# Twelve weight slabs of the first projection stored in another column order and read back by other access patterns

## What is computed

```python
SPLIT_SIZES = (ML_QK, ML_QK, ML_WIDTH, ML_WIDTH, ML_WIDTH, ML_HEADS, ML_HEADS,
               HG_FDIM, HG_FDIM, HG_WIDTH, HG_WIDTH)
...
        u = rmsnorm(h, norm_w[l])
        proj = jnp.einsum('bsd,dc->bsc', u, w_in[l].astype(jnp.float32))
        (ml_q, ml_k, ml_v, ml_o, ml_z, ml_i, ml_f,
         hg_q, hg_f, hg_i, hg_g) = jnp.split(proj, split_points, axis=-1)
```

## Time and profile before

| | |
|---|---|
| runs | 1983.43 and 1983.77 us, median 1983.6 |
| span of the profiled execution | 1982.4 us (the runs are 1.0 and 1.4 us above it) |
| PE busy | 1973.1 us, 100% |
| PE weight loads (beside the matmuls) | 1642.8 us, 83% |
| DVE busy | 1476.6 us, 74% |
| ACT busy | 1147.5 us, 58% |
| DMA | 535.95 MB, mean 270 GB/s |
| matmuls | 9126, of them 1536 in the 16 slabs of phase A |

### The profile page before, as it was taken

The page is one execution under the profiler, slowest core; times in us unless marked ns, Lnnn a source line. Parts: engine busy times, 40 slices in busy tenths (PEclk is TensorE's granted clock), DMA queues, the critical chain, the costliest instruction groups (busy, mean ns, idle before and its releaser), DMA issues.

```text
span 1982.4 us, 23547 instructions
## 1 busy us (share of the span) xinstructions
PE 1973.1 (100%) x9126; PEld 1642.8 (83%) x9126; DVE 1476.6 (74%) x1571; ACT 1147.5 (58%) x1417; POOL 114.5 (6%) x140
## 2 busy tenths in 40 slices
PE   9999999999999999999999999999999999999999
PEld 7888888888888888888888888888888888888887
DVE  6877776555666666768888657888988898888764
ACT  7546444554466455556666445666666666666553
POOL 1000010000001110000000000000000000000000
PEclk9999999999999999999999999999999999999999
DMA  9788798999889999858797876788878887877553
GB/s 377 255 250 278 234 322 275 323 327 313 278 287 298 342 341 299 255 195 253 283 299 244 313 242 238 236 299 278 273 229 303 271 264 240 308 251 235 209 178 125
DMA packets 86816, 535.95 MB, mean 270 GB/s; under 512 B 10417, under 2 KB 11185, under 8 KB 40753
## 3 DMA queue, kind: packets, MB, share of 16 engines
q1 hardware_dynamic: 72736, 458.69, 60.9%
q0 software_dynamic: 13824, 75.50, 20.0%
q10 hardware_dynamic: 144, 0.26, 0.0%
HBM read 529.69 MB, written 105.38 MB: 320 GB/s over the span
## 4 chain that ended last, share of the span: by engine, by line
PE 96%; DVE 2%; DMA 1%; ACT 1%; issue 0%; SPq 0%; DVEq 0%; ACTq 0%
PE acc L1342 45%; PE acc L1347 22%; PE aux L1699 15%; PE aux L1703 8%; PE aux L1325 1%; PE aux L1415 1%; DMA raw<-in_w_in 1%; DVE wlo L1851 1%; PE aux L1780 0%; DVE wlo L2507 0%; ACT whi L915 0%; PE aux L1405 0%; PE aux L1430 0%; DVE att_z L2353 0%; PE aux L1316 0%
## 5 line engine op out<-in xcount | busy, mean ns | idle before, releaser
L1851 DVE TENSOR_TENSOR wlo<-raw,whi 128x1024 fp32r<-128x1024 f32 x512 | 624.2, 1225 | 359.7 <-ACT whi L915 350.2
L915 ACT ACTIVATE whi<-raw 128x1024 fp32r<-128x1024 f32 x511 | 537.3, 1058 | 535.0 <-PE acc L1347 490.0
L1342 PE MATMUL acc<-whi,actA_hi 128*128 128x512 f32 x892 | 351.6, 394 | 0.0
L1342 PE MATMUL acc<-whi,actA_lo 128*128 128x512 f32 x892 | 347.4, 390 | 0.0
L1342 PE MATMUL acc<-whi,actB_hi 128*128 128x512 f32 x796 | 312.7, 393 | 0.2 <-DVE actB_lo L2624 0.2
L1342 PE MATMUL acc<-whi,actB_lo 128*128 128x512 f32 x796 | 309.9, 389 | 0.0
L1164 ACT ACTIVATE whi<-ple 128x1024 fp32r<-128x1024 f32 x192 | 202.3, 1060 | 136.0 <-PE acc L1347 87.4
L2507 DVE TENSOR_TENSOR wlo<-ple,whi 128x1024 fp32r<-128x1024 f32 x192 | 231.9, 1223 | 37.6 <-ACT whi L1164 30.6
L1347 PE MATMUL acc<-wlo,actA_hi 128*128 128x512 f32 x892 | 238.7, 389 | 0.0
L1347 PE MATMUL acc<-wlo,actB_hi 128*128 128x512 f32 x796 | 213.2, 390 | 1.2 <-DVE wlo L1851 1.2
L2507 DVE TENSOR_TENSOR wlo<-raw,whi 128x1024 fp32r<-128x1024 f32 x144 | 175.4, 1223 | 36.1 <-ACT whi L1164 30.9
(11 more groups left out here) (360 smaller groups left out, 2391.9 us busy)
## 6 DMA issues: line engine op xcount, KB each, us to landing
raw<-in_w_in SPq DMA_DIRECT2D x108, 1024.0 KB, 7.6
raw<-in_w_ffn_out SPq DMA_DIRECT2D x44, 1024.0 KB, 7.0
summed<-in_w_ffn_in POOLq DMA_DIRECT2D x36, 1024.0 KB, 11.9
raw<-in_w_ffn_in SPq DMA_DIRECT2D x72, 512.0 KB, 7.5
ple<-summed SPq DMA_DIRECT2D x24, 1024.0 KB, 4.8
raw<-summed SPq DMA_DIRECT2D x48, 512.0 KB, 4.8
ple<-in_w_ffn_in SPq DMA_DIRECT2D x18, 1024.0 KB, 7.6
ple<-in_w_ffn_in POOLq DMA_DIRECT2D x36, 512.0 KB, 9.8
```

The source lines that it names most:

```text
L915: act.activation(whi[:, g % RING], raw_piece(g), ACT.Copy).then_inc(hi_ready, 1)
L1342: pe.matmul(acc2(n)[:, t, :], act[x][:, k + c, t * P:(t + 1) * P], whi[:, g % RING, c, :], start=(p == 0 and c == 0 and x == 0), stop=False)
L1851: dve.tensor_tensor(wlo[:, g % RING], raw_piece(g), whi[:, g % RING].bitcast(F32), ALU.subtract)\
```

## The change

The host now stores the columns of slabs 1 to 7 and 9 to 13 in another order within the slab, the same in every row. The table `READ_ORDER` gives three numbers h, g, e for a slab: the 512 columns are seen as g groups of h runs of e columns, and stored with the h index outermost. The matmul's moving operand is the same 512 words of `whi` or `wlo`, now walked in the order g, h, e, which is the reference's order again. So for slab 9, (2, 256, 1), word 0 is followed by word 256, then 1, then 257; for slab 10, (256, 2, 1), by words 2, 4, up to 510, and then the odd ones; for slab 1, (2, 64, 4), four words are read at 0, four at 256, four at 4, and so on. Slabs 0, 8, 14 and 15 and all other weights are read as before. On each engine the instructions, their order and their waits stay as they are, 96 matmuls of each of the twelve slabs have the new pattern.

```diff
--- before.py
+++ after.py
@@ -79,6 +79,19 @@
 
 HG_START = (23, 49)
 X_SQUARES = 11
+
+READ_ORDER = {1: (2, 64, 4), 2: (2, 32, 8), 3: (2, 16, 16), 4: (2, 8, 32), 5: (4, 32, 4), 6: (2, 128, 2), 7: (8, 16, 4),
+              9: (2, 256, 1), 10: (256, 2, 1), 11: (4, 8, 16), 12: (16, 8, 4), 13: (2, 4, 64)}
+
+
+def in_read_order(x, order):
+
+    h, g, e = order
+    if order == (256, 2, 1):
+        return x.rearrange("p (g h) -> p h g", h=2)
+    if e == 1:
+        return x.rearrange("p (h g) -> p g h", h=h)
+    return x.rearrange("p (h g e) -> p g h e", h=h, g=g)
 ATT_START = (35, 55)
 
 
@@ -1330,6 +1343,11 @@
                 if u >= 4:
                     aux_taken(pe, u - 4)
 
+            def moving(ring, n, g, c):
+
+                x = ring[:, g % RING, c, :]
+                return in_read_order(x, READ_ORDER[n]) if n in READ_ORDER else x
+
             def piece(n, p, act, k, last, i=0, slabs=0):
 
                 g = SLABS[n][p]
@@ -1339,12 +1357,12 @@
                 for c in range(PK):
                     for t in range(T):
                         for x in range(2):
-                            pe.matmul(acc2(n)[:, t, :], act[x][:, k + c, t * P:(t + 1) * P], whi[:, g % RING, c, :],
+                            pe.matmul(acc2(n)[:, t, :], act[x][:, k + c, t * P:(t + 1) * P], moving(whi, n, g, c),
                                       start=(p == 0 and c == 0 and x == 0), stop=False)
                 pe.wait_ge(lo_ready, g + 1 + i * ROUND)
                 for c in range(PK):
                     for t in range(T):
-                        ins = pe.matmul(acc2(n)[:, t, :], act[0][:, k + c, t * P:(t + 1) * P], wlo[:, g % RING, c, :],
+                        ins = pe.matmul(acc2(n)[:, t, :], act[0][:, k + c, t * P:(t + 1) * P], moving(wlo, n, g, c),
                                         start=False, stop=(last and c == PK - 1))
                 ins.then_inc(piece_used, 1)
 
@@ -2770,7 +2788,15 @@
     for name in _WEIGHTS:
         laid[name] = blocks(inputs[name][0])
     w = inputs["w_in"][0]
-    laid["w_in"] = blocks(np.concatenate([w[:, :MI], w[:, HQ:]], axis=1))
+    laid["w_in"] = blocks(np.concatenate([w[:, :MI], w[:, HQ:]], axis=1)).copy()
+    for s, (h, g, e) in READ_ORDER.items():
+        slab = A_COLS[s] // COLS if A_COLS[s] < MI else (A_COLS[s] - HQ) // COLS + MI // COLS
+        x = laid["w_in"][slab]
+        if (h, g, e) == (256, 2, 1):
+            x = x.reshape(*x.shape[:-1], 2, 256).swapaxes(-1, -2)
+        else:
+            x = x.reshape(*x.shape[:-1], g, h, e).swapaxes(-2, -3)
+        laid["w_in"][slab] = x.reshape(laid["w_in"][slab].shape)
     laid["w_in_gates"] = w[:, MI:HQ].reshape(KD, P, HQ - MI).transpose(1, 0, 2)
     for name in ("w_pe", "w_ple_2"):
         laid[name] = short(inputs[name][0])
```

## The result

The changed kernel takes 2033.5 us in the median of 2 runs (2032.37 and 2034.70), 1.0244 of the time before, with a 95% interval of 1.0227 to 1.026. That is 49.9 us more, where 20.5 were forecast. The time lies inside the range (1982.5 to 2046), but it is slower by more than the 2% that the forecast kept within, between rivals B2 (2024.6) and B (2045.0). What the profile shows is none of the cases.

A forecast was written before the change was run, and what follows sets the result against it. PE was taken to bound the kernel, busy 1973.1 of 1982.4 us. Span 1982.4 plus 20.5 for slab 9, 0 for all else, gave 2002.9; with 1.2 us above the span, 2004.1 us; range 1982.5 to 2046.

The forecast's parts named there:

- B2: Moving reads of slabs 9 and 10 double, slab 6 is free: +41.0 us, 2024.6 us, 2.07% slower; chance 0.08.
- B: Moving reads with runs under four columns (slabs 6, 9, 10) double, 20.5 us each: 2045.0 us, 3.1% slower; chance 0.17.
- What bounds the kernel: PE busy 1973.1 of 1982.4 us at full clock, so slower matmuls in the first projection lengthen the whole run.
- the zeros for loads, splits, outputs and storage: DMA loads, ACT and DVE splits and PSUM outputs of the rearranged slabs were each priced at cost 0.
- The price of a slab that can't be fed: Streaming part of a slab's 96 matmuls doubles, 213.3 ns more each: 20.5 us a slab.
- Which slabs?: Slab 9 alone, having no column near its predecessor, pays +20.5 us (ends 0 and +31.4); the other eleven pay 0.
- The other floor: Line 1627's matmuls, with one jump in the moving operand, last 377 to 379 ns: one jump costs nothing that shows.
- A gain is excluded: PE already takes a column per cycle in the matmuls, so the lower end of the change's cost is 0.
- A: PE's moving reads run ahead far enough to hide single words, so the change costs nothing: 1983.6 us; chance 0.24.
- C: Each jump between runs in the twelve slabs costs 0.417 ns: 77.8 us more, 2061.4 us, 3.9% slower; chance 0.08.
- D: Every rearranged slab doubles, as PE reads ahead only along the stored row: 245.8 us more, 2229.4 us; chance 0.05.
- The test named in the prediction: If slabs 1, 5, 7 and 12 part from each other, distance counts, not the run, and no case is right.

## Why the prediction was wrong

*What bounds the kernel* held: what the slabs lost went to the end undiminished, 48.0 us in the slabs and 48.2 in the span. So did the zeros for loads, splits, outputs and storage (the ratio of the version that is only stored in the new orders is 1.000), and PE's waits did not grow.

*The price of a slab that can't be fed* was right in size: 20.5 us forecast, 21.5 measured for slab 10. The rows that it was taken from, a write of DVE that doubled with runs under four words, may have nothing to do with it: as far as the runs show, the agreement in size is luck. The factor of two here is that of one word for each line and reader.

**The step that failed is "Which slabs?"** I gave the doubling to slab 9, as the walk farthest from every free row, and zero to the eleven others. The runs showed the opposite: slab 9 gains 1.1 us, slab 10 loses 21.5, slab 6 9.9, and eight others 0.8 to 4.7 each, 17.7 together (slab 11 in part by its low clock). The nearness of two successive columns was the wrong measure. Every second column is what counts: slab 9's are neighbours, slab 10's are four words apart. That rule accounts for these two slabs; the other 27.6 us, of slab 6 and the eight others, are shown to lie in the walk (but for the 1.6 of slab 11's low clock), and why each costs what it does stays open (below). The free reads of DVE by every other word could not carry the argument to PE, as I had said myself of their pace, and then used them all the same to put slab 10 among the free.

The other floor, that a jump costs nothing at line 1627, could not carry it either. I compared durations, which I had just said are not the price, and these matmuls are of another kind: their operands are plain float32 (`sgu_v`, `wsT`), not float32r, and their starts are 0.215 us apart for 256 columns (eight take 1.89 us), 0.84 ns a column, half the pace of the matmuls that were changed. A slower read could hide behind that.

```profile
832.58 1.89 PE L1627 MATMUL aux<-sgu_v,wsT 128*128 128x256 f32 x8
```

*"A gain is excluded"* failed as well, in a small thing. I had 13.4 ns a matmul beyond the 512 columns in hand and took them as fixed. 11 of them hang on the walk, and over the whole program they are 4% of the time.

*The rule of the Trainium skill* (SBUF — State Buffer, section "Door 1: The DMA port swizzle", on lines of 16 bytes and two hits in one) gave slab 9 as the payer, too. The trace disagrees: 216 ns there, and 451 in slab 10, which has two hits in each line, one after the other. The measurement decides. With "two hits" counted for every second column, the rule's number two fits the walks of single words: one gives 451, two 227. The stricter sentence on the same page, a penalty at each crossing, fails in slab 9, which crosses with each column.

*The rivals.* A, no cost, is out. B had slabs 6, 9 and 10 doubled: two of the three lose, 9 does not. B2 had slab 10 right and slabs 6 and 9 wrong; its 2024.6 us was nearest in time, by the wrong sum. C, a price by jump, would give slab 9 its 20.5. D is out with slab 13. The test named in the prediction, that slabs 1, 5, 7 and 12 part from each other, came true (2.3, 3.4, 4.7, 1.9 us), and with it that none of the cases had it. But they do not differ "in their jump alone", as I wrote: they have 2, 4, 8 and 16 rows in turn, so the test does not single out the distance.

**What stays open.** Slabs 1 to 5, 7 and 12 have two words in a line for each reader and should take 227 ns by the rule; they take 236 to 278. In the run with other distances, runs of 4 took 225 ns with 32 rows 16 words apart and 232 with 64 rows 8 apart. Whether the distance between rows or their number makes these differences, which stay within about 50 ns, no run separates.

The six walks with runs of 2 (431 to 487 ns) all have four lines or more for each reader, which puts them in the slow group, but no order within it was found. Nor was the reason why slab 6, where each reader takes turns between two lines and finds two words in each, takes 332 ns, between the two levels, or why four rows in turn take 268 to 283 and not 216.

There is no measurement of a walk of the output in PSUM in place of the order in memory, nor of an odd number of rows in turn. And no walk was shifted by a word or two, so that the groups of four words are aligned ones is assumed.

## What to carry to other kernels

With float32r operands, look at every second column of the moving operand, not at neighbours. In these runs of 512 columns, one of its words in a group of four doubled the matmul, two in succession gave the contiguous pace or, in runs with jumps, up to about 50 ns more, and four in succession saved 11 ns. This kernel, whose PE is never idle, took 80 us less (4%) with its weights stored as two rows and walked in turn; 7 us more of waits were the one cost that showed. And where a trace has a remainder per instruction beyond the array's time, price it as something that could move either way; I took it for a constant.

## What the runs showed of the hardware that was not expected

- A contiguous float32r walk is not the fastest: 227 ns for 512 columns against 216 for two rows in turn, and at 384 columns the difference is nearly the same (173 against 163), so it doesn't go with the columns.
- Each of the two streams of columns can take turns, by single words, between two or three groups of four words at 0.52 to 0.60 ns a column; with four or more it takes 0.84 to 0.95.
- The clock fell to its lower level for about 3 us in slab 11 in eight of nine profiles, in one of them with slab 11 read in a row, and not in the profile of the kernel before. Such a stretch cost 1.6 us (slab 11 stored in the new order, read in a row) and 1.7 us (all weights from two rows).
